# A two-layer streaming encoder in one core: block turns between the weight splits, six load buffers for four, and pooling sums with zero-padded buffers

## The reference

```python
for l in range(DEPTH):                       # DEPTH = 2, D_MODEL = 1024, D_FF = 2816, SEQ = 256
    x = layer_norm(ALPHA * x + 0.5 * swiglu(x, ffn1_w13[l], ffn1_w2[l]), ln_g[l, 0], ln_b[l, 0])
    h = x @ w_in[l]                          # [pool 256 | c_q 256 | c_kv 128 | k_pe 64]
    y_pool = pool_mixer(u_pool, pool_w[l], pool_scale[l])
    y_mla = mla_mixer(c_q, c_kv, k_pe, positions, ...)     # 6 heads, chunk-causal
    x = layer_norm(ALPHA * x + concat([y_pool, y_mla]) @ w_out[l], ln_g[l, 1], ln_b[l, 1])
    x = layer_norm(ALPHA * x + memory_cross_attention(x, mem, ...), ln_g[l, 2], ln_b[l, 2])
    x = layer_norm(ALPHA * x + 0.5 * swiglu(x, ffn2_w13[l], ffn2_w2[l]), ln_g[l, 3], ln_b[l, 3])
```

## Time and profile before

| what | value |
|---|---|
| runs (3) | median 1093.1 us, 1093.0 to 1094.49 |
| the profiled execution's own time | 1093.56 us |
| its span | 1091.7 us |
| granted TensorE clock, mean | 0.999 |
| TensorE matmuls busy | 1081.4 us (99%), 5720 |
| VectorE busy | 847.9 us (78%) |
| ScalarE busy | 534.4 us (49%) |
| GpSimd busy | 80.8 us (7%) |
| DMA | 203.18 MB, mean 186 GB/s |

### The profile page before, as it was taken

One profiled execution on the slowest core, in us unless ns is written; L12 is line 12 of the kernel. 1 busy time (PEld: TensorE's weight loads), 2 busy tenths in 40 slices (PEclk: granted clock), 3 DMA queues, 4 the chain that ended last, 5 costly groups with the idle time before them and its releaser, 6 DMA issues.

```text
span 1091.7 us, 16584 instructions
## 1 busy us (share of the span) xinstructions
PE 1081.4 (99%) x5720; PEld 934.6 (86%) x5720; DVE 847.9 (78%) x1450; ACT 534.4 (49%) x731; POOL 80.8 (7%) x120
## 2 busy tenths in 40 slices
PE   9999999999999999999999999999999999999997
PEld 8788888999999888888888888889999988888885
DVE  5888877797765778778687887878977777887885
ACT  5545444556464554444454444445664646444442
POOL 0260000140100100000010000001401000000000
PEclk9999999999999999999999999999999999999999
DMA  8666766354664475665666557554446555556551
GB/s 301 194 210 193 230 194 220 112 166 163 198 207 149 154 231 177 214 188 179 210 191 222 173 184 226 169 194 124 162 155 205 182 171 193 177 189 214 174 188 58
DMA packets 156803, 203.18 MB, mean 186 GB/s; under 512 B 12656, under 2 KB 137840, under 8 KB 156752
## 3 DMA queue, kind: packets, MB, share of 16 engines
q1 hardware_dynamic: 153552, 193.25, 55.0%
q0 software_dynamic: 2912, 8.92, 2.7%
q10 hardware_dynamic: 288, 0.33, 0.1%
HBM read 201.41 MB, written 1.05 MB: 185 GB/s over the span
## 4 chain that ended last, share of the span: by engine, by line
PE 96%; DVE 2%; issue 1%; DMA 0%; ACT 0%; POOLq 0%; DVEq 0%; SPq 0%; POOL 0%
PE ps L591 93%; PE ps L674 1%; DVE w_lo L1429 1%; DVE hidden_T L1486 0%; PE ps L1118 0%; DMA raw<-in_ffn_w 0%; PE ps L854 0%; DVE memT L1462 0%; DVE mixT L1492 0%; PE ps L942 0%; PE ps L1088 0%; PE ps L995 0%; PE ps L1047 0%; DVE x L1535 0%; PE ps L1049 0%
## 5 line engine op out<-in xcount | busy, mean ns | idle before, releaser
L1180 ACT CAST w_hi<-raw 128x1024 fp32r<-128x1024 f32 (+1 forms) x247 | 255.8, 1044 | 213.2 <-PE ps L591 97.3
L1429 DVE TENSOR_TENSOR w_lo<-raw,w_hi 128x1024 fp32r<-128x1024 f32 (+1 forms) x247 | 295.7, 1222 | 77.7 <-ACT w_hi L1180 75.9
L591 PE MATMUL ps<-w_hi,xT 128*128 128x512 f32 (+1 forms) x912 | 287.1, 389 | 0.0
L591 PEld LDWEIGHTS ps<-w_hi,xT 128*128 128x128 f32 x912 | 171.0, 188 | 35.1 <-issue 0.4
L591 PE MATMUL ps<-w_hi,mixT 128*128 128x512 f32 x688 | 198.1, 390 | 0.5 <-DVE mixT L1492 0.5
L1180 ACT CAST v_flat<-raw 128x1024 fp32r<-128x1024 f32 (+1 forms) x114 | 118.5, 1045 | 138.5 <-DMA raw<-in_ffn_w 70.0
L1486 DVE STREAM_TRANSPOSE hidden_T<-ev 32x128 f32<-32x128 f32 x576 | 174.4, 303 | 8.6
L591 PE MATMUL ps<-v_flat,xT 128*128 128x512 f32 (+1 forms) x660 | 177.2, 389 | 0.0
L591 PE MATMUL ps<-w_lo,xT 128*128 128x512 f32 (+1 forms) x456 | 175.3, 388 | 0.0
L591 PEld LDWEIGHTS ps<-w_hi,mixT 128*128 128x128 f32 x688 | 128.7, 188 | 27.3 <-DVE v_flat L1429 1.0
L591 PEld LDWEIGHTS ps<-v_flat,xT 128*128 128x128 f32 x660 | 123.7, 188 | 25.4 <-DVE cqp L1429 0.2
(11 more groups left out here) (168 smaller groups left out, 1224.6 us busy)
## 6 DMA issues: line engine op xcount, KB each, us to landing
raw<-in_ffn_w SPq DMA_DIRECT2D x352, 256.0 KB, 3.7
raw<-in_ffn_w SPq DMA_DIRECT2D x88, 512.0 KB, 5.1
raw<-in_mem_wkv SPq DMA_DIRECT2D x32, 512.0 KB, 4.8
raw<-in_w_out SPq DMA_DIRECT2D x16, 512.0 KB, 4.1
raw<-in_mem_wq SPq DMA_DIRECT2D x16, 512.0 KB, 5.6
raw<-in_mem_wo SPq DMA_DIRECT2D x16, 512.0 KB, 4.7
gb<-in_ln_g POOLq DMA_DIRECT2D x8, 512.0 KB, 4.3
gb<-in_ln_b POOLq DMA_DIRECT2D x8, 512.0 KB, 6.1
```

The source lines that it names most:

```text
L591: return nc.tensor.matmul(dst, stand, move, start=start, stop=stop, skip_group_check=True)
L1180: nc.scalar.copy(slot_hi[slot[n]][:, 0:size], raw[:, n % RAW, 0:size]).then_inc(hi_done, 1)
L1429: nc.vector.tensor_tensor(slot_lo[slot[n]][:, s], raw[:, n % RAW, s], slot_hi[slot[n]][:, s].bitcast(F32), ALU.subtract).then_inc(lo_done, 1)
```

## The change

Nine things are edited together.

1. `RAW` goes from 4 to 6. Unit n's load waits for the split of unit n - 6. Room comes from `gains` (one layer's rows in place of two), the constants (197 columns for 673) and `poolM`, which becomes a view of `hidden_T`.
2. Step 0 of the FFNs after the first is turned by VectorE, as the middle steps are; TensorE's four transposes there go.
3. The 16 block transposes of a step are issued in four groups of four, each followed by one weight split, in place of all in a row behind the multiply.
4. The pooling buffers have eight zero columns ahead of each tile, so that one addition serves all tokens; the copies of the tokens without a partner go. The sums stay undivided: ScalarE takes the pool bank a second time, scaled by the window (`poolW`), the first 16 tokens are corrected by a factor, and the division is in `pool_scale`.
5. `rope_q` of block 0 waits for both takings of the pool bank.
6. The rope's angles are computed in `pw` (before it is cleared and loaded) and later, behind unit 23 in place of 11.
7. The small loads are reordered; the row gains are loaded a layer at a time.
8. `load_gains` issues four DMAs of 256 KB in place of two of 512 KB, and each waits for a unit of TensorE's.
9. `center` waits for four DMAs a norm.

```diff
-RAW = 4
+RAW = 6
...
-        def by_blocks(s):
+        def by_blocks(e, s):
 
-            return 0 < s < FS - 1
+            return e + s > 0 and s < FS - 1
...
-                        if j == 1 and s == 1:
+                        if j == 1 and s == 1 and e == 0:
                             turn_hidden(0)
...
-                nc.scalar.copy(poolU, two(bank(m))).then_inc(pool_taken, 1)
+                nc.scalar.copy(poolU[:, :, PAD:PAD + S], two(bank(m))).then_inc(pool_taken, 1)
+                ahead_to(plan["uqC", l]["units"] + 3)
+                act.wait_ge(consts_landed, 16)
+                for t in range(2):
+                    last = nc.scalar.mul(poolW[:, t, :], two(bank(m))[:, t, :], cst[:, C_WIDE + t:C_WIDE + t + 1])
+                last.then_inc(pool_taken, 1)
...
-                ahead_to(u + 7) if e == 0 else ahead(("hidden", e, 0))
+                if e == 0:
+                    ahead_to(u + 7)
+                else:
+                    for i in range(P // BLOCK):
+                        turn_blocks(0, i)
+                        if i % 2:
+                            ahead_to(u + 8 + i // 2)
                 split_hidden(0)
...
-                        for n in range(first + 6 * s, first + 6 * s + 4):
-                            split_lo(n, it)
+                        for i in range(4):
+                            turn_blocks(s + 1, i, it)
+                            split_lo(first + 6 * s + i, it)
                         split_hidden(s + 1, it)
...
-                    dve.wait_ge(gains_landed, 32 * (e + 1))
+                    dve.wait_ge(gains_landed, 64 * (e + 1))
...
                 if b == 0:
-                    dve.wait_ge(pool_taken, l + 1)
+                    dve.wait_ge(pool_taken, 2 * l + 2)
...
             def load_gains(e):
+                l, k = e // 4, e % 4
+                first, apart = {0: (plan["ffn", l, 0]["units"] + (41 if e == 0 else 5), 3), 1: (plan["wout", l]["units"], 1),
+                                2: (plan["wq", l]["units"], 2), 3: (plan["ffn", l, 1]["units"] + 5, 3)}[k]
                 for i, w in enumerate(("ln_g", "ln_b")):
-                    pool.dma_start(gb[:, i, :], a[w][e // 4, e % 4:e % 4 + 1, :].partition_broadcast(P))\
-                        .then_inc(gains_landed, 16)
+                    for c in range(HALVES):
+                        cols = slice(c * D // 2, (c + 1) * D // 2)
+                        pool.wait_ge(pe_done, done["unit", first + apart * (2 * i + c)])
+                        pool.dma_start(gb[:, i, cols], a[w][l, k:k + 1, cols].partition_broadcast(P))\
+                            .then_inc(gains_landed, 16)
...
-                    own(nc.gpsimd.tensor_tensor(dst[:, tiles_, shift:S], src[:, tiles_, shift:S],
-                                                src[:, tiles_, 0:S - shift], ALU.add))
-                    own(nc.gpsimd.tensor_copy(dst[:, tiles_, 0:shift], src[:, tiles_, 0:shift]))
+                    own(nc.gpsimd.tensor_tensor(dst[:, tiles_, PAD:], src[:, tiles_, PAD:],
+                                                src[:, tiles_, PAD - shift:PAD + S - shift], ALU.add))
...
-                own(nc.gpsimd.tensor_tensor(poolM[:, :, :], poolM[:, :, :], inv_count, ALU.mult))
-                nc.gpsimd.tensor_tensor(poolB, poolM[:, :, :], poolU, ALU.subtract).then_inc(pooled, 1)
+                early = poolM[:, :, 0:EARLY]
+                own(nc.gpsimd.tensor_tensor(early, early, early_share, ALU.mult))
+                pool.wait_ge(pool_taken, 2 * l + 2)
+                nc.gpsimd.tensor_tensor(poolM, poolM, poolW, ALU.subtract).then_inc(pooled, 1)
...
             clear_keys()
-            pool.wait_ge(pe_done, done["unit", plan["ffn", 0, 0]["units"] + 11])
+            pool.wait_ge(pe_done, done["unit", plan["ffn", 0, 0]["units"] + 23])
...
+                pool.wait_ge(norm_done, normed(4 * l, 1, 1))
                 pool_group(l)
                 pool.wait_ge(pool_split, l + 1)
+                if l < L - 1:
+                    load_row_gains(l + 1)
                 load_gains(4 * l + 1)
```

More of the change, by code:

```diff
@@ L212, in plan_ffn @@
         for s in range(1, FS):
-            marks += [UNIT_] * 2 + ([[("hidden", e, 0)]] if s == 1 else []) + (turned(2) + turned(3) if e == 0 and s == 1 else [])
+            marks += [UNIT_] * 2 + ([[("hidden", e, 0)]] if e == 0 and s == 1 else []) + (turned(2) + turned(3) if e == 0 and s == 1 else [])
             marks += [UNIT_, ["U", "I", "I"]] + [UNIT_] * (2 * (s < FS - 1))
@@ L994, in mix @@
                 for t in range(2):
[L995 removed]
+                    last = nc.tensor.matmul(pool_bank[:, t, :], pw[:, l, t, :], poolM[:, t, :],
                                             start=t == 0, stop=True, skip_group_check=True)
@@ L1520, in ffn @@
                 state["next"] = first + LOOP_UNITS * LOOPS
-                ahead(("unit", plan["ffn", l, w]["units"] + 6 * (FS - 1) - 2 + 1))
+                for i in range(P // BLOCK):
+                    turn_blocks(FS - 2, i)
+                    ahead_to(first + LOOP_UNITS * LOOPS + min(i + 1, 3))
+                ahead(("unit", u + 6 * (FS - 1) - 2 + 1))
                 split_hidden(FS - 2)
-                ahead(("item", m + 2 * FS - 1))
+                ahead_to(u + 6 * FS)
                 multiply(FS - 1)
@@ L1848, in pool_group @@
             def pool_group(l):
-                pool.wait_ge(pool_taken, l + 1)
+                for padded in (poolU, poolA, poolB):
+                    own(nc.gpsimd.memset(padded[:, :, 0:PAD], 0.0))
+                pool.wait_ge(pool_taken, 2 * l + 1)
                 src = poolU
@@ L1870, in _ @@
             rope_angles()
+            for l in range(L):
+                for t in range(2):
+                    pool.dma_start(pscale[:, l, t:t + 1], a["pool_scale"][l, t * P:(t + 1) * P].rearrange("(p o) -> p o", o=1))\
+                        .then_inc(pscale_landed, 16)
+            load_row_gains(0)
+            load_gains(0)
+            pool.wait_ge(tables_done, 1)
+            own(nc.gpsimd.memset(pw[:, :, :, :], 0.0))
             for l in range(L):
@@ L1874, in _ @@
                     pool.dma_start(pw[rows, l, g // 2, rows], a["pool_w"][l, g]).then_inc(small_landed, 16)
-                for t in range(2):
-                    pool.dma_start(pscale[:, l, t:t + 1], a["pool_scale"][l, t * P:(t + 1) * P].rearrange("(p o) -> p o", o=1))\
-                        .then_inc(small_landed, 16)
-                for dst, w in ((gains[:, l, 0:Q_LORA], "q_norm_g"), (gains[:, l, Q_LORA:Q_LORA + KV_LORA], "kv_norm_g")):
-                    pool.dma_start(dst, a[w][l:l + 1, :].partition_broadcast(P)).then_inc(small_landed, 16)
-            pool.wait_ge(tables_done, 1)
-            load_gains(0)
+            pool.wait_ge(pscale_landed, 16 * 2 * L)
+            for l in range(L):
+                own(nc.gpsimd.tensor_tensor(pscale[:, l, :], pscale[:, l, :], cst[:, C_THIN:C_THIN + 2], ALU.mult))
             for l in range(L):
```

98 lines of the change are left out of this document (52 added, 46 removed).

## The result

| | before | after |
|---|---|---|
| median of the runs | 1093.38 us (5 runs) | 1104.55 us (5 runs, 1104.13 to 1106.0) |
| span of the profiled execution | 1091.7 us | 1102.4 us |
| granted TensorE clock, mean | 0.999 | 0.995 |

The ratio is 1.0103, with a 95% interval from 1.0088 to 1.0118: the change costs 11.2 us. The direction was forecast, at 1099.2 us; the time is outside the forecast range, which ended at 1102.6.

What follows compares the result with a forecast made beforehand. TensorE was taken as the bound, busy 1081.4 of 1091.7 us. Terms -1.3 - 0.7 + 0.1 + 8.0 = +6.1 gave 1099.7 us, or 1099.2 for the median; range 1096.4 to 1102.6.

Steps and rivals of the forecast that it cites:

- step 4: Norm behind the mixing, both layers: fourth gain load asked for too late, center and TensorE's turn wait; +4.0 each, +8.0.
- Step 1: FFNs after the first: four step 0 transposes move from TensorE to VectorE, 0.44 us saved three times; -1.3 us.
- The cover: Second FFN: VectorE's added block transposes and splits finish before TensorE wants the hidden columns, 1.2 us to spare; cost 0.
- Step 2: First FFN: two more load buffers remove ScalarE's wait for data, so TensorE's stall for the hidden split goes; -0.7 us.
- Step 3: Pooling sums and rope's wait for both pool bank takings, second layer: bounds -0.3 and +0.6, taken as +0.1 us.
- the wait on the second taking: Second layer's rope: VectorE's sine product slips 0.6 us behind ScalarE's second pool bank copy; held certain.
- the slow split: Second layer's weight split, 2.06 us beside a GpSimd addition: may be quick again (-0.8) or not.
- the gains come later still: Norm behind the mixing: landing takes 4.3 to 6.1 us or more, or block 1's chain loses too; 1102 to 1105; chance 0.11.

Runs made afterwards that it cites:

- the experiment: Changed kernel with all four gain loads behind the mixing at the first wout mark, plus step 0's hidden transposes given back to TensorE in all FFNs: 1094.31 us.
- that last kernel: Changed kernel with only the fourth half load of the gains behind the mixing asked for at mark y, block 0's sum: 1100.08 us, ratio 1.0059.

## Why the prediction came out too low

The place, the sign and the chain of step 4 were right; two terms of the sum, steps 3 and 4, were mis-sized, and step 4 mainly by a mechanism that I had not counted, the clock. The median came out 5.4 us above the forecast; between the two traces TensorE's last matmul moved by 10.2 where the sum has 6.1, so the sum was 4.1 too low.

**Step 1, three turns: right.** Forecast -1.3, measured -1.35 in the trace and 1.24 by the experiment. The cover held as well: in the second FFN VectorE's hidden split ends at 396.01 (395.33 + 0.68) and TensorE wants it at 396.87, 0.9 to spare where I had 1.2.

**Step 2, the stall in the first FFN: right**, -0.8 for -0.7. The traces bear out its reason too. In the chain that ended last of the kernel before, this load is on the path:

```profile
31.90 3.65 DMA raw<-in_ffn_w
35.58 1.06 ACT w_hi L1180
```

In the changed kernel the same load (the 24th DMA of these weights) is issued at 23.25 and lands at 29.40. ScalarE rounds it at 32.03 without a wait, so the wait of 1.63 is gone, and VectorE's multiply comes at 35.45 instead of 37.80. The waits for loads that ScalarE still has, 1.08 and 0.95 us, stand before later splits than the one that the multiply is behind. Timeline of the changed kernel:

```profile
35.45 0.68 DVE L1479 TENSOR_TENSOR ev<-ps,ev 128x512 f32<-128x512 f32 x1
35.62 1.05 ACT L1184 CAST w_hi<-raw 128x1024 fp32r<-128x1024 f32 x1 [1.08 <-DMA raw<-in_ffn_w]
...
46.16 0.69 DVE L1500 TENSOR_TENSOR mixT<-hidden_T,mixT 128x512 fp32r<-128x512 f32 x1
```

**Step 3, the pooling: the term was too small**, +0.1 for +1.35. I took the wait on the second taking as certain and the slow split as a coin's toss, and let the two nearly cancel. The runs weigh them the other way: moving the sums takes away 1.9 (1093.07 to 1091.2), putting the takings together a further 0.4, in all 2.3; 1.0 of that was in the kernel before already, and the 1.3 left is the term. I had also looked at one split and not at the queue behind it, where `memK` stands. The Trainium skill, "SBUF — State Buffer", section "Who interferes with whom", says that a VectorE instruction with two inputs in SBUF contends with a GpSimd instruction that reads SBUF, and one with a single such input does not. The trace agrees on both: the split grows from 1.22 to 2.32 us beside the subtraction, while the cosine product, with one input in PSUM, keeps its 0.54 beside the copy at 772.69. But neither engine is held up for the whole of the other's instruction, as the prediction had it: the subtraction took 1.30 without a split beside it (in the run with the sums later) and 1.90 with one. The rule had been cited, and priced at 0.6 at one place; it should have been applied to every split beside the sums.

**Step 4, the fourth gain load: the mechanism right, the term 4.0 for 5.55 and 5.64 a norm.** It has two errors. (a) The landing: I had 3.15 us from issue to `center`; it is 3.65. The load is also issued 0.2 behind ScalarE's copy at the same mark (282.61 against 282.40), where I had 0.1. From `center` on my working was exact: 2.95 forecast to the turn, 2.93 measured. So the wait is 4.3, where I had 3.7, and 0.3 more for the second half of the turn. The Trainium skill, "DMA: Bandwidth & Descriptors", section "Anatomy of one DMA", gives 2.6 for this load, an estimate: the lone load here took 1 us more, and those beside weight loads 6 to 8. (b) The clock, left out altogether: behind a wait of 4.2 us TensorE runs 3.3 us at 1.2 GHz. The stretch costs +1.46 and +1.54. At full clock it would have cost 0.28 (from the run with TensorE kept busy), so the clock's part is 1.2 a norm, of which 0.22 comes back at block 1's turn: some 2.0 in all, as keeping TensorE busy brought (2.05, or 1.6 from trace to trace), and half of the 4.1 us by which the sum was too low. The landing and issue make another 1.2 of them, the pooling the last 1.25, and the small terms give back 0.4. The Trainium skill, "TensorE: Matmul & The Clock Gate", section "HAM oscillation — how this bites in real kernels", has it that a wait for a transfer throttles the array, and that the price is half the throttled time: by that rule 1.7 for each stretch of 3.4 us, an estimate; the trace has 1.46 and 1.54, and 0.3 us of each stretch falls into the wait, so it agrees. The row that I needed was in sight: the kernel before shows a mean clock of 0.999, and I never asked whether it would hold across the wait that I was predicting.

The rival "the gains come later still" had the right range, 1102 to 1105, for a mostly wrong reason: the landing cost 0.5 more, not 1 to 3, and the clock, which it does not name, did the rest. That its range was met is luck.

## What to carry to other kernels

Where a change makes a saturated TensorE wait for several microseconds, price the wait and then the clock behind it: here 4.2 us of waiting cost 5.6. A load with a mark must be asked for by the time that it takes beside its neighbours (8 us here), not by what it takes alone (3.6), and a mark's place is to be looked up in the order that the engine runs, where "the next unit" was 11 us away. And an engine with little to do is not free: ask what its instructions stretch on the others, and whether they can be run a few microseconds later.

## What the runs showed of the chip

- The granted clock fell behind waits of 4.2 us (four times, in two kernels) and of 3.00 us (once), not behind one of 2.34 us, nor where matmuls without use filled the wait. Each time it was back after one stretch of 3.4 us. In the changed kernel it fell about when TensorE resumed; behind the wait of 3.00 us it fell 1.3 us after that. Executions of that last kernel differ in their mean clock (0.998, 0.997, 0.995) and their time with it (1098.82, about 1100, 1101.29).
- A VectorE split of 1.22 us took 1.64 beside a GpSimd addition and copy and 2.32 beside a GpSimd subtraction with two inputs; that subtraction took 1.90 there, and 1.30 with no split beside it.
- The same 256 KB broadcast took 3.65 us from issue to its reader with little else in flight, 5.9 with five weight loads issued in the 8 us before it, and about 8 as the second of two.
